# Where the gains of the two feed-forward norms are multiplied in: from the activations on VectorE to the gate and up weights on ScalarE

## What is computed

```
x += 0.5 * swiglu(rmsnorm(x, norm_ffn1));  x += hybrid_mixer(rmsnorm(x, norm_mix))
x += 0.5 * swiglu(rmsnorm(x, norm_ffn2));  y  = rmsnorm(x, norm_final)

rmsnorm(x, gain) = x * rsqrt(mean(x * x) + 1e-6) * gain            # gain: one number per column of x
swiglu(h, w_gate, w_up, w_down) = (silu(h @ w_gate) * (h @ w_up)) @ w_down      # 1024 -> 2816 -> 1024
```

## Time and profile before

| | |
|---|---|
| three runs, median (lowest to highest) | 2298.25 us (2289.78 to 2298.78) |
| the profiled execution | 2298.98 us, span 2297.2 us, mean clock 0.986 |
| TensorE busy | 2228.9 us, 97% |
| TensorE weight loads busy | 2008.5 us, 87% |
| VectorE busy | 1411.6 us, 61% |
| ScalarE busy | 811.9 us, 35% |
| GpSimd busy | 314.6 us, 14% |
| first gate/up product | 46.1 us from the start |

### The profile page before, as it was taken

The page is one execution under the profiler, slowest core; times in us unless marked ns, Lnnn a source line. Parts: engine busy times, 40 slices in busy tenths (PEclk is TensorE's granted clock), DMA queues, the critical chain, the costliest instruction groups (busy, mean ns, idle before and its releaser), DMA issues.

```text
span 2297.2 us, 35167 instructions
## 1 busy us (share of the span) xinstructions
PE 2228.9 (97%) x13488; PEld 2008.5 (87%) x13488; DVE 1411.6 (61%) x2361; ACT 811.9 (35%) x1566; POOL 314.6 (14%) x296
## 2 busy tenths in 40 slices
PE   4999999999999999999999999899999999999998
PEld 3999999999888877876778878799999999988887
DVE  7655556555575776765654674855555555557576
ACT  6322222222343446644442322522222222233343
POOL 6100011000100002200001213511112111110000
PEclk7999999999999999999998999999999999999999
DMA  3232232232775655623225673132232232277554
GB/s 130 72 102 78 79 100 89 95 101 77 254 258 186 193 161 137 191 82 99 90 93 169 214 236 126 58 96 77 78 102 85 92 108 78 78 281 261 170 189 166
DMA packets 246981, 306.10 MB, mean 133 GB/s; under 512 B 23968, under 2 KB 159648, under 8 KB 246816
## 3 DMA queue, kind: packets, MB, share of 16 engines
q1 hardware_dynamic: 238176, 290.75, 39.6%
q10 hardware_dynamic: 8640, 13.11, 1.6%
HBM read 209.43 MB, written 91.10 MB: 131 GB/s over the span
## 4 chain that ended last, share of the span: by engine, by line
PE 88%; DVE 7%; issue 1%; DMA 1%; ACT 1%; POOL 0%; SPq 0%; DVEq 0%; POOLq 0%; ACTq 0%
PE ps L2187 15%; PE ps L2189 15%; PE ps L2188 15%; PE ps L2197 7%; PE ps L2198 7%; PE ps L2199 7%; PE ps L2118 4%; PE ps L2120 4%; PE ps L2119 4%; PE ps L2373 1%; DVE gla_s L2002 1%; PE ps L2345 1%; PE ps L2353 1%; PE ps L2136 1%; PE ps L2137 1%
## 5 line engine op out<-in xcount | busy, mean ns | idle before, releaser
L2187 PE MATMUL ps<-hs,w_hi 128*128 128x384 f32 (+1 forms) x1232 | 381.4, 310 | 4.8 <-DVE first_u L1695 2.9
L2188 PE MATMUL ps<-hs,w_hi 128*128 128x384 f32 (+1 forms) x1232 | 380.6, 309 | 0.0
L2189 PE MATMUL ps<-hs,w_lo 128*128 128x384 f32 (+1 forms) x992 | 306.6, 309 | 0.0
L2197 PE MATMUL ps<-w_hi,dh 128*128 128x512 f32 x770 | 300.8, 391 | 2.0 <-DVE w_lo L1749 0.8
L2199 PE MATMUL ps<-w_hi,dh 128*128 128x512 f32 x770 | 299.7, 389 | 0.0
L1647 DVE TENSOR_TENSOR w_lo<-w_raw,w_hi 128x512 fp32r<-128x512 f32 x178 | 134.3, 755 | 180.2 <-ACT w_hi L1180 177.7
L2187 PEld LDWEIGHTS ps<-hs,w_hi 128*128 128x128 f32 x1232 | 233.4, 189 | 5.9 <-issue 5.9
L2198 PE MATMUL ps<-w_lo,dh 128*128 128x512 f32 x610 | 237.3, 389 | 0.0
L1180 ACT CAST w_hi<-w_raw 128x512 fp32r<-128x512 f32 x220 | 135.7, 617 | 283.1 <-PE ps L2189 280.3
L2188 PEld LDWEIGHTS ps<-hs,w_hi 128*128 128x128 f32 x1232 | 233.7, 190 | 0.0
L1746 DVE TENSOR_TENSOR dh<-dr,dh 128x640 fp32r<-128x640 f32 x154 | 126.8, 823 | 167.0 <-ACT dh L1211 167.0
(11 more groups left out here) (258 smaller groups left out, 4612.6 us busy)
## 6 DMA issues: line engine op xcount, KB each, us to landing
dr<-hid_mid SPq DMA_DIRECT2D x154, 320.0 KB, 3.1
w_raw<-in_w_ffn_down SPq DMA_DIRECT2D x176, 256.0 KB, 3.5
hid_mid<-st SPq DMA_DIRECT2D x88, 320.0 KB, 2.2
w_raw<-in_w_ffn_gate SPq DMA_DIRECT2D x44, 512.0 KB, 5.1
w_raw<-in_w_ffn_up SPq DMA_DIRECT2D x44, 512.0 KB, 5.1
hid_mid<-sg SPq DMA_DIRECT2D x66, 320.0 KB, 2.2
hq<-o_mid SPq DMA_DIRECT2D x70, 128.0 KB, 3.3
w_raw<-in_w_in SPq DMA_DIRECT2D x14, 512.0 KB, 5.0
```

Of the source, the lines that this page charges most:

```text
L2187: mm(out, hi[:, k, :], b_hi, start=k == 0 and j in (GP1, GP6, GP5), stop=False, skip_group_check=True)
L2188: mm(out, hi[:, k, :], b_lo, start=False, stop=False, skip_group_check=True)
L2189: last = mm(out, lo[:, k, :], b_hi, start=False, stop=k == 3, skip_group_check=True)
L2197: mm(out, hi, w_h, start=first and p in D_FRESH, stop=False, skip_group_check=True)
```

## The change

The two gains are no longer broadcast. Two loads of 8x128 numbers (`gain_rows`) bring both behind the identity matrix; TensorE transposes them in one instruction and ScalarE copies the result to `gains`, one number per partition for each of the 8 blocks of the contraction, for both norms. `norm_scale` on VectorE multiplies by the root alone, a TENSOR_SCALAR in place of a SCALAR_TENSOR_TENSOR. ScalarE gets `g_scale`: for each unit eight ACTIVATEs of 128x128, in place in `w_raw`, with the gain as the scale; it counts a new semaphore, `block_scaled`, on which casts and sums wait instead of on the load. The first two sums of a pair move on VectorE from behind the split of GP1's block to ahead of the split of GP6's. The broadcast load of the second gain and three waits of SP ahead of it go.

```diff
@@ SP
             load_x(0)
-            sp.dma_start(gain_first, norm_ffn1.rearrange("a (h n) -> a h n", h=2).to_broadcast([P, 2, HALF])
-                         ).then_inc(gain_loaded, 16)
             load_x(5)
-            sp.dma_start(ident[:, :], c_ident).then_inc(ident_loaded, 16)
+            sp.dma_start(ident[:, :], c_ident).then_inc(gain_loaded, 16)
+            for f, g in enumerate((norm_ffn1, norm_ffn2)):
+                sp.dma_start(gain_rows[KT * f:KT * (f + 1), :], g.rearrange("a (k p) -> (a k) p", p=P)
+                             ).then_inc(gain_loaded, 16)
             load_x(1)
...
-            sp.wait_ge(G["decay"], 2 * GLA_HEADS)
-            sp.wait_ge(G["qe"], GLA_HEADS)
-            sp.wait_ge(G["vT"], NCH * GLA_HEADS)
-            load_gain(gain2[:, :], norm_ffn2[0:1, :])
@@ ScalarE
+            def g_scale(f, q, e):
+                raw = g_raw(f, q, e)
+                act.wait_ge(*g_loaded(f, q, e))
+                for k in range(KT):
+                    nc.scalar.activation(raw[:, k, :], raw[:, k, :], ACT.Copy, scale=gains[:, f, k:k + 1]).then_inc(B["scaled"], 1)
...
                 if j == GP1:
-                    act.wait_ge(*g_loaded(f, q, 0))
+                    act.wait_ge(*g_scaled(f, q, 0))
                 if j == GP4:
-                    act.wait_ge(*g_loaded(f, q, 1))
+                    act.wait_ge(*g_scaled(f, q, 1))
...
                         if s + G_LEAD < G_STEPS:
+                            q, j = divmod(s + G_LEAD, NP)
+                            if j == GP6:
+                                g_scale(f, q, 1)
                             g_hi(f, s + G_LEAD)
+                            if j == GP3 and q + 1 < G_PAIRS:
+                                g_scale(f, q + 1, 0)
...
             norm_squares(0, 0)
+            act.wait_ge(gains_set, 1)
+            nc.scalar.copy(gains[:, :, :], ps[:, 3, 0:2 * KT].rearrange("p (f k) -> p f k", f=2)).then_inc(gains_set, 1)
...
                 norm_blocks(0, i)
+                if i == 0:
+                    g_scale(0, 0, 0)
...
                 if i == 0:
+                    g_scale(0, 0, 1)
                     g_hi(0, 0)
...
                 norm_sums(1, i - 1)
+                if i < 3:
+                    g_scale(1, 0, i - 1)
@@ VectorE
-                dve.wait_ge(gain_loaded, 16 * (2 * f + 1))
...
-                v.scalar_tensor_tensor(out=xs_norm(f, n), in0=x_norm(f, t), scalar=rstd[:, 2 * f, t:t + 1], in1=gain,
-                                       op0=ALU.mult, op1=ALU.mult).then_inc(N["scaled"], 1)
+                v.tensor_scalar(xs_norm(f, n), x_norm(f, t), rstd[:, 2 * f, t:t + 1], None, ALU.mult).then_inc(N["scaled"], 1)
...
                 if j == GP1:
-                    dve.wait_ge(*g_loaded(f, q, 1))
+                    dve.wait_ge(*g_scaled(f, q, 1))
...
             def g_prepare(f, s):
+                if s % NP == GP6:
+                    g_sums(f, s - GP6)
                 g_lo(f, s)
-                g_sums(f, s)
+                if s % NP in (GP2, GP4):
+                    g_sums(f, s)
@@ TensorE
-            pe.wait_ge(ident_loaded, 16)
+            pe.wait_ge(gain_loaded, 16 * 3)
+            nc.tensor.transpose(ps[:, 3, 0:2 * KT], gain_rows, ident[0:2 * KT, 0:2 * KT]).then_inc(gains_set, 1)
```

More of the change, by code:

```diff
@@ L175, in build @@
         expo = sb("expo", [P, TT])
+        gains = sb("gains", [P, 2, KT])
         gla_gain = sb("gla_gain", [P, 1])
@@ L192, in build @@
         junk2 = place(10240, "junk2", [P, D_MODEL], BF16)
-        gain2 = place(13824, "gain2", [P, D_MODEL])
         st2 = place(17920, "st2", [P, 4, HTOK])
@@ L333, in xs_first @@
             return piece(4, 3 + n % 4)
-        gain_first = piece(4, 2)
+        gain_rows = hs_f[0:2 * KT, 2, 0, 4, 0:P]
         P1, U2, U3 = (p1_1, p1_2), (u2_1, u2_2), (u3_1, u3_2)
@@ L418, in build @@
         x_spilled = [sem(f"x_spilled{j}") for j in range(2)]
-        ident_loaded = sem("ident_loaded")
         gain_loaded = sem("gain_loaded")
         expo_set = sem("expo_set")
+        gains_set = sem("gains_set")
         def named(prefix, names):
@@ L431, in build @@
         S = named("gateup", "done kept added silu mult gated")
-        B = named("block", "summed hi lo")
+        B = named("block", "scaled summed hi lo")
         W = named("down", "summed a_hi a_lo step tile p1_kept added")
@@ L530, in g_loaded, with g_scaled @@
             return w_loaded[u % RAW], loads(u)
+        def g_scaled(f, q, e):
+            return B["scaled"], KT * (2 * (G_PAIRS * f + q) + e + 1)
         def two_places(a, b):
@@ L1237, in _ @@
             norm_squares(0, 0)
+            act.wait_ge(gains_set, 1)
+            nc.scalar.copy(gains[:, :, :], ps[:, 3, 0:2 * KT].rearrange("p (f k) -> p f k", f=2)).then_inc(gains_set, 1)
             norm_squares(0, 1)
+            act.wait_ge(gains_set, 2)
             for i in range(HT):
                 norm_blocks(0, i)
+                if i == 0:
+                    g_scale(0, 0, 0)
                 if i + 2 < HT:
@@ L1568, in scale @@
                 dve.wait_ge(N["root"], 2 * t + 2)
-                dve.wait_ge(gain_loaded, 16 * (n + 1))
+                dve.wait_ge(gain_loaded, 16 * (n // 2 + 4))
                 v.scalar_tensor_tensor(out=out, in0=x_res(n // 2, t), scalar=rstd[:, n, t:t + 1],
@@ L1595, in norm_scale @@
                 dve.wait_ge(N["root"], 2 * n + 2)
-                dve.wait_ge(gain_loaded, 16 * (2 * f + 1))
                 if f:
                     dve.wait_ge(x_spilled[n % 2], 16 * (HT + n // 2 + 1))
-                    gain = gain2[:, :].rearrange("p (h n) -> p h n", h=2)
-                else:
-                    if n >= 4:
-                        dve.wait_ge(N["turned"], 4 * (n // 2 - 1))
-                    gain = gain_first
-                v.scalar_tensor_tensor(out=xs_norm(f, n), in0=x_norm(f, t), scalar=rstd[:, 2 * f, t:t + 1], in1=gain,
-                                       op0=ALU.mult, op1=ALU.mult).then_inc(N["scaled"], 1)
+                elif n >= 4:
+                    dve.wait_ge(N["turned"], 4 * (n // 2 - 1))
+                v.tensor_scalar(xs_norm(f, n), x_norm(f, t), rstd[:, 2 * f, t:t + 1], None, ALU.mult).then_inc(N["scaled"], 1)
             def norm_scales(f, i):
@@ L1796, in gate_up @@
                         dve.wait_ge(ld_const, 16 * N_CONST_LD)
-                        dve.wait_ge(ident_loaded, 16)
+                        dve.wait_ge(gain_loaded, 16 * 3)
                         v.tensor_copy(ident_bf[:, :], ident[:, :]).then_inc(const_set, 1)
@@ L2239, in d_tail @@
                 last.then_inc(W["tile"], 1)
-            pe.wait_ge(ident_loaded, 16)
+            pe.wait_ge(gain_loaded, 16 * 3)
+            nc.tensor.transpose(ps[:, 3, 0:2 * KT], gain_rows, ident[0:2 * KT, 0:2 * KT]).then_inc(gains_set, 1)
             for i in range(4):
+                if i == 1:
+                    pe.wait_ge(gains_set, 2)
                 norm_turn(0, i)
```

## The result

The changed kernel takes 2306.84 us (median of 20 runs, 2296.57 to 2314.43), the kernel before, measured beside it, 2297.85 us (20 runs, 2288.02 to 2301.05): ratio 1.0042, 95% interval 1.0030 to 1.0053. It is about 9 us slower. I had forecast 2296, within half a per cent of no change; it is still within it, but on the other side, and outside my range.

A forecast was written before the change was run, and what follows sets the result against it. It took TensorE to bound the gate/up stages and VectorE the two entries. Terms of -2.3, -1.3 and +0.7 us summed to -2.9 from the profiled 2298.98 us, less 0.7 to the runs' median: forecast 2296 us, range 2288 to 2304.

The forecast's parts named there:

- rival 2: Gate/up, each of 44 pairs: a scaling unit over 3.7 us stalls TensorE; 2330 us, mild form 2305 to 2311; chance 7%.
- Step 1: VectorE's norm multiplications, 10 per norm: 0.75 us alone, 1.60 beside GpSimd, saving 0.53 us each.
- step 4: Start of the first norm: earlier loads and cheaper multiplications bring TensorE's chain forward; -2.3 us (-5.7 to +1.2).
- rival 1: Norm entries: the new multiplication gains nothing beside GpSimd, waiting up to one 1.29 us subtraction; 2299 us; chance 20%.
- Step 2: In-place scaling on ScalarE, 704 instructions: 0.39 us each, 2.4 us a unit, about 200 us more on ScalarE.
- Step 3: Inside the gate/up stages: scaling fits each pair except one late load that stalls TensorE; +0.7 us (0 to +3.1).
- slack of 3.7: Gate/up pairs: scaling a unit may take 3.7 us before TensorE waits for VectorE's eviction; 2.4 and 3.1 fit.
- third group of seven: First norm: VectorE's third group of seven normed-tile subtractions was to start at 37.1 us instead of 38.44.
- fourth group: First norm: VectorE's fourth group of normed-tile subtractions was to start near 45.7 us instead of 47.98.
- Step 5: Start of the second norm: three cheaper multiplications on the chain to TensorE's last wait; -1.3 us (0 to -2.7).

The follow-up runs named there:

- e1: The kernel before with one unused tile of 64 bytes per partition where the changed kernel has `gains`; 2303.64 us, ratio 1.0021.
- e2: The changed kernel with `gains` allocated last, so every other tile lies as in the kernel before; 2299.27 us, ratio 1.0002.
- e12: The kernel before with only the norm multiplication changed to TENSOR_SCALAR, the feed-forward gains applied nowhere; 2283.49 us, ratio 0.9951.
- e4: e2 without the 704 scaling ACTIVATEs, so the two gains are applied nowhere; 2290.36 us, ratio 0.9969.
- e9: e2 with each scaling ACTIVATE of 128 columns cut into two of 64; 2325.01 us, ratio 1.0130.
- e3: The kernel before with 32 unused bytes per partition where the changed kernel has `gains`; 2308.51 us, ratio 1.0036.
- e7: e3 with the tiles of the down projections, `dh` among them, another 96 bytes on; 2304.76 us, ratio 1.0032.
- e15: The kernel before with `sinks` and `neg_sinks` allocated ahead of `w_raw`, moving the weight tiles 64 bytes on; 2286.96 us, ratio 0.9954.
- e8: The changed kernel with `hs` and `hq` 96 and `dh` 128 bytes from their places in the kernel before; 2323.52 us, ratio 1.0118.
- e10: e3 run once more, unchanged, for another trace; 2304.62 us (one run).
- e17: e2 with the late unit scaled by VectorE instead of ScalarE, in the layout of e16; 2275.57 us, ratio 0.9912.
- e16: e15 with `dh` and its neighbours in the first feed-forward moved 64 bytes on as well; 2271.09 us, ratio 0.9898.

## Why the prediction was wrong

What failed is a term that the sum doesn't contain, put at nothing without a reason: the products in the stages that the change leaves alone. I read "TensorE is busy for 524.41 of 525.00" as "nothing there can change", and stages that the diff doesn't touch as fixed. The new tile moved their operands against each other, and the price of one product isn't fixed: **+8.3 us** (e1), from down projections that are some 6 and 7 us longer and gate/up stages that are some 3 us shorter each. No rival of mine had it either; rival 2's 2305 to 2311 met the time by luck, with another mechanism.

Without the shift the change costs +0.7 us (e2, standard error 0.7), where my sum was -2.9: that alone would have stayed inside my range. Step by step:

*Step 1.* Right. Alone 0.75 us (743 and 753 ns in the rows above), beside GpSimd 1.67 each (3.32 and 3.11 for two in a row), where I took 1.60; the softmax rows were a good base. Why it is 1.67 shows when GpSimd's rows of after are laid beside VectorE's, which stand under step 4:

```profile
41.87 1.72 POOL L1020 TENSOR_TENSOR hs<-first_t,hs 128x512 fp32r<-128x512 f32 x1
43.55 1.73 POOL L1020 TENSOR_TENSOR hs<-first_t,hs 128x512 fp32r<-128x512 f32 x1
45.23 1.74 POOL L1020 TENSOR_TENSOR hs<-first_t,hs 128x512 fp32r<-128x512 f32 x1
```

These end at 43.59, 45.28 and 46.97 us, and VectorE's three at 44.14, 45.82 and 47.53: each some 0.55 us behind the one of GpSimd, and GpSimd's next 1.14 or 1.15 behind VectorE's. The two take turns. The Trainium skill ("SBUF — State Buffer", section "Who interferes with whom") says that the later of the two blocks fully until the earlier ends, and this trace agrees. But the wait isn't a whole subtraction of 1.29 us, as rival 1 had it. VectorE's instruction starts while GpSimd's is under way and waits for the rest of it, and a turn of both takes 1.67 to 1.69. The old multiplication took turns as well. Before:

```profile
32.14 1.28 POOL L1018 TENSOR_TENSOR hs<-first_t,hs 128x512 fp32r<-128x512 f32 x1
32.47 2.04 DVE L1604 SCALAR_TENSOR_TENSOR hs_f<-hs_f,rstd 128x1024 f32<-128x1024 f32 x1
```

It ended 1.09 us behind GpSimd's (34.51 and 33.42), where the new one ends 0.55 behind: the 0.53 apiece that I took, beside GpSimd too. e12 gains 3.4 us in all.

*Step 2.* Right: 389 ns each, 2.45 us a unit, ScalarE 1015.0 us busy.

*Step 3.* Right in kind. Steady pairs pay nothing (two take 49.19 us in e2), the late unit pays: TensorE's wait at 77 us is 2.41 in e2, 1.83 before, nothing in e4. The slack of 3.7 was too large (e9). But the late unit of each stage's second pair was my step 4's, where I wrote that nothing of the gain is lost.

*Step 4* is the one mis-sized: -2.3 forecast. Up to the third group of seven it holds: 36.84 us, forecast 37.1, and the first product comes at 44.50 instead of 46.09, 1.6 earlier. The fourth group I put at 45.7; it starts at 47.45, against 47.98 before. VectorE's timeline of after shows why:

```profile
42.38 1.76 DVE L1621 TENSOR_SCALAR hs_f<-hs_f,rstd 128x1024 f32<-128x1024 f32 x1
44.06 1.76 DVE L1663 TENSOR_TENSOR w_lo<-w_raw,w_hi 128x512 fp32r<-128x512 f32 x1
45.75 1.78 DVE L1663 TENSOR_TENSOR w_hi<-w_sum,w_hi 128x512 fp32r<-128x512 f32 x1
47.45 0.67 DVE L1641 TENSOR_TENSOR first_t<-first_t,ps 128x512 f32<-128x512 f32 x1
```

The two splits behind the multiplications took 0.68 us each before. Having moved forward, they now stand beside GpSimd, take turns with it and last 1.76 and 1.78: 2.2 us lost. The two sums that the change moved did the same (1.74 and 1.63 instead of 1.75 and 0.69). I had priced contention for the instruction that changes and left its neighbours at their old durations. TensorE's next wait, for ScalarE's eviction `first_p`, ends at 52.30 us instead of 52.83: 0.5 is left, and the late unit takes that.

*Step 5.* Right up to the late unit, which it didn't have. TensorE's long waits of the second entry add up to 6.6 us before and to 4.7 in e2: 1.9 less, where I had 1.3. Then comes one more of 1.41 that the scaled late unit brings (1507.92 us in e2), and 0.5 is left. The gain can't be put down to the multiplication alone, since e12 doesn't show it there.

In full-clock spans the parts are: new multiplication -3.4 (e12), order of sums, loads and waits -2.3 (e4 less e12), scaling +6.4 (e2 less e4), layout +8.3 (e1). Sum +9.0, of 9.1 measured; the first three add up to e2's +0.7 by the way they are taken, and the layout is measured apart from them. The scaling is the largest of them on the change's own side: I had 0.7 for it in step 3, and what it costs at the start stood inside step 4's gain. Of the 6.4, 1.8 is the later first product (42.77 us in e4, 44.56 in e2), 2.4 the wait at 77 us, 1.4 the one at 1508. The remaining 0.8 is within the uncertainty.

What stays open is why the distance between the operands in SBUF sets the pace of products. The runs show that it does, that it is the same again after 256 and 512 bytes but not after 128, that it has a sign, and that each pair of operands has its own; no view of the profile shows a wait for it.

## What to carry to other kernels

Before crediting or blaming a change, compare the spacing of the same products in a stage that it doesn't touch; if that moved, look at what the change allocates. A small tile belongs behind the large ones, or ahead of all, and the distance between weight and activation tiles is a setting worth trying by itself: here it is worth 14.5 us by the full-clock span (0.6%), more than the change was ever meant to bring. And when an instruction moves forward, price its neighbours anew, for what they now stand beside.

## What the runs showed of the hardware that I had not expected

- Spacing of 128x512 products, the moving operand weights, the stationary one `dh`: 0.2267 us at the old distance and at 256 and 512 bytes from it, 0.2333 at +32, +64 and +128 (e3, e1, e7), 0.2289 at -64 (e15), in each case at a granted clock of 1.00.
- A pair of gate/up, by change of distance between weights and inputs: 24.59 us at 0, 24.45 at +64, 24.92 at +96 (e8, which has the change too), 24.08 at -64; at +32 three values, 24.36, 24.45 and 24.64, two of them in one stage of one execution (e10).
- A TENSOR_SCALAR of 128x1024 or a TENSOR_TENSOR of 128x512 from two SBUF tiles, on VectorE beside GpSimd's subtractions of two SBUF tiles: the engines take turns of 1.67 to 1.69 us, against 0.75 and 0.68 us for the VectorE instruction alone.
- Span times mean granted clock repeats to 1.4 us over runs of the kernel before whose times lie 22 us apart, which made effects of 2 us readable where ratios had intervals of 4. It doesn't in every layout: the standard deviation is 3.4 us in e3, 4.5 in e7, 3.5 in e15 and 5.1 in e17.
- The mean granted clock itself differs between kernels in a way that I can't explain: about 0.986 on average in most, 0.9905 in the 6 runs of e12 and 0.9902 in those of e16.
